# Hymba-style decoder step with PEER experts: one set of products for the sample values, residual transposed into PSUM and added at the end, gate loads moved ahead, and stores of the result by row tile

## The reference, cut to what matters

```python
xn = rms_norm(x, norm1_g)                       # 576 x 1024
q, k, v, glu = project(xn, w_in)                # 8 query heads, 2 key heads of 64
a = sliding_window_attention(q, k, v, sinks)    # prompt: blocks of 128; sample: 128 cached keys + 8 new
c = conv_module(glu)                            # depthwise conv, layernorm, swish, pointwise
h = x + concat(rms_norm(a), rms_norm(c)) @ w_out
xt = rms_norm(h)
# PEER: 8 heads, each takes 16 of 128 x 128 experts by two lists of 128 keys
idx, gate = product_key_top16(xt @ wq, keys)
hu  = sum_d u[idx, d] * xt[d]                   # first table
act = gelu(hu) * gate
y   = h + sum_k act[k] * v[idx[k], :]           # second table
```

## Time and profile before

| | us |
|---|---|
| median of 3 runs (lowest, highest) | 1780.7 (1778.49, 1786.08) |
| profiled execution | 1786.37 |
| its span | 1784.6 |
| PE busy | 1659.4 (93%) |
| VectorE (DVE) busy | 1432.4 (80%) |
| ScalarE (ACT) busy | 781.7 (44%) |
| GpSimd (POOL) busy | 574.3 (32%) |

### The profile page before, as it was taken

One profiled execution on the slowest core, in us unless ns is written; L12 is line 12 of the kernel. 1 busy time (PEld: TensorE's weight loads), 2 busy tenths in 40 slices (PEclk: granted clock), 3 DMA queues, 4 the chain that ended last, 5 costly groups with the idle time before them and its releaser, 6 DMA issues.

```text
span 1784.6 us, 23135 instructions
## 1 busy us (share of the span) xinstructions
PE 1659.4 (93%) x8377; PEld 1417.5 (79%) x8377; DVE 1432.4 (80%) x2697; ACT 781.7 (44%) x1310; POOL 574.3 (32%) x395
## 2 busy tenths in 40 slices
PE   7886989899999899998999999998999989999997
PEld 5765645578699899998999999997777778777786
DVE  2558577865787687889889999838989989899897
ACT  3221230331135444447889999843333333333332
POOL 0000000000000232334555655524545556456462
PEclk9999999989999999999999999999999999999999
DMA  6110603115345689897999999999999999999996
GB/s 198 48 48 0 75 12 103 63 49 178 104 130 142 229 284 303 291 296 261 366 365 397 406 385 370 358 379 377 403 404 395 403 402 375 404 403 404 403 384 214
DMA packets 155320, 482.39 MB, mean 270 GB/s; under 512 B 25999, under 2 KB 43087, under 8 KB 153031
## 3 DMA queue, kind: packets, MB, share of 16 engines
q1 hardware_dynamic: 99911, 279.57, 44.6%
q0 software_dynamic: 55296, 201.35, 29.9%
HBM read 426.17 MB, written 54.42 MB: 269 GB/s over the span
## 4 chain that ended last, share of the span: by engine, by line
PE 49%; DMA 19%; DVE 19%; ACT 7%; issue 4%; SPq 1%; DVEq 0%; ACTq 0%
PE ps L786 19%; DMA raw<-in_v 12%; DMA gelu_matrix<-gest 7%; PE ps L936 6%; PE ps L740 6%; DVE acc L1656 5%; PE ps L550 5%; PE ps L566 4%; DVE lo L1491 3%; PE ps L914 3%; ACT hi L1053 2%; DVE cacc L1346 2%; ACT Gs L1228 2%; DVE al L1778 2%; ACT gA L1212 1%
## 5 line engine op out<-in xcount | busy, mean ns | idle before, releaser
L1274 POOL DMA_INDIRECT ring<-in_u,idx x192 | 280.7, 1462 | 953.5 <-DVE ijg L1632 579.8
L1491 DVE TENSOR_TENSOR lo<-raw,hi 128x1024 fp32r<-128x1024 f32 x256 | 312.9, 1222 | 154.1 <-ACT hi L1053 152.6
L1053 ACT ACTIVATE hi<-raw 128x1024 fp32r<-128x1024 f32 x256 | 270.6, 1057 | 361.0 <-DMA raw<-in_v 185.8
L1274 POOL DMA_INDIRECT ring<-in_v,idx x192 | 292.2, 1522 | 226.0 <-DVE acc L1656 216.4
L786 PE MATMUL ps<-xh,hi 128*128 128x384 f32 x1024 | 350.6, 342 | 7.8 <-DVE lo L1491 7.8
L786 PE MATMUL ps<-xh,lo 128*128 128x384 f32 x1024 | 343.6, 336 | 0.0
L786 PE MATMUL ps<-xl,hi 128*128 128x384 f32 x1024 | 343.6, 336 | 0.0
L936 PE MATMUL ps<-hi,ah 128*128 128x512 f32 x768 | 243.5, 398 | 29.3 <-DVE al L1778 26.7
L1656 DVE SCALAR_TENSOR_TENSOR acc<-ring,hu,acc 128x1024 f32<-128x1024 f32 x192 | 245.1, 1277 | 0.1
L936 PE MATMUL ps<-lo,ah 128*128 128x512 f32 x768 | 238.9, 393 | 0.0
L936 PE MATMUL ps<-hi,al 128*128 128x512 f32 x768 | 238.3, 392 | 0.0
(11 more groups left out here) (211 smaller groups left out, 1978.9 us busy)
## 6 DMA issues: line engine op xcount, KB each, us to landing
raw<-in_uT SPq DMA_DIRECT2D x128, 512.0 KB, 6.8
raw<-in_v SPq DMA_DIRECT2D x128, 512.0 KB, 9.2
wring<-in_wblk SPq DMA_DIRECT2D x58, 512.0 KB, 3.6
gelu_matrix<-gest SPq DMA_DIRECT2D x64, 384.0 KB, 8.9
gate_matrix<-Gs SPq DMA_DIRECT2D x16, 1536.0 KB, 8.5
Gl<-gate_matrix SPq DMA_DIRECT2D x64, 384.0 KB, 11.5
gel<-gelu_matrix SPq DMA_DIRECT2D x64, 384.0 KB, 8.8
wring<-in_wblk SPq DMA_DIRECT2D x16, 256.0 KB, 2.6
```

The lines of the kernel that those rows point to most:

```text
L1053: nc.scalar.activation(hi[:, s % 2, :], raw[:, s % RAWS, :], ACT.Copy).then_inc(s_hi, 1)
L1274: pool.indirect_dma_start(ring[:, r % SLOTS, :], None, table, bass.IndirectOffsetOnAxis(idx[:, t, c:c + 1], 0)).then_inc(g_in[r % SLOTS], 16)
L1491: nc.vector.tensor_tensor(lo[:, s % 2, :], raw[:, s % RAWS, :], hi[:, s % 2, :].bitcast(F32), ALU.subtract).then_inc(s_lo, 1)
```

## The change

1. `sample_values`: eight matmuls, one for each sequence, with all 128 value columns and the weights of both key heads (64 columns of output), and one matmul of 512 columns that adds the new values for all. Half of each result is not used: VectorE takes the rows and columns of each key head in a copy of its own.
2. The residual: TensorE transposes h into `ps[0..2]`, ScalarE copies it back over the dense part of `hT` (now by tokens), the first value products start the sums, and the residual is added by VectorE when PSUM is emptied, whole row tiles at a time. ScalarE has no part in that.
3. SyncE waits for the gate block and loads the first gates and the first GELU pair ahead of `after_u(123)`; the next three pairs follow one by one.
4. The gathered rows of v are all done by value tile 124 (`V_ROWS_END`), and the sample's upper half is released there.
5. The dense result is stored as three row tiles, each as soon as it is added.

```diff
+V_ROWS_END = NKEY - 4
 def v_rows(n):
-    return V_ROW0 + n * (NROW - V_ROW0) // NKEY
+    return V_ROW0 + min(n, V_ROWS_END) * (NROW - V_ROW0) // V_ROWS_END
...
+            sp.wait_ge(s_gst, 16 * NBLK)
+            load_gelu(0)
+            for b in range(0, NBLK, 2):
+                load_gates(0, b)
             for n in range(U_TAIL, NKEY):
                 after_u(n)
-                if n == U_TAIL + 1:
-                    sp.wait_ge(s_gst, 16 * NBLK)
-                    for b in range(0, NBLK, 2):
-                        load_gates(0, b)
-                    for k in range(EP):
-                        load_gelu(k)
+                if n - U_TAIL < EP - 1:
+                    load_gelu(n - U_TAIL + 1)
...
-            sp.wait_ge(s_yd, 2 * DTI)
-            sp.dma_start(y_d[0:DT, :].rearrange("(t p) d -> p t d", p=P), ring[:, 0:DTI, :]).then_inc(s_out, 16)
-            sp.wait_ge(s_out, 48)
+            for t in range(DTI):
+                sp.wait_ge(s_yd, t + 1)
+                sp.dma_start(y_d[t * P:(t + 1) * P, :], ring[:, t, :]).then_inc(s_out, 16)
+            sp.wait_ge(s_out, 16 * (2 + DTI))
...
                 for b in range(NDB):
-                    for g in range(NKV):
-                        grp, slot = b // 2, (b % 2) * 2 + g
-                        rows = slice(g * HD, (g + 1) * HD)
-                        c = grp * P + slot * 32
-                        nc.tensor.matmul(out[rows, b * 32:b * 32 + 32], cv[:, b, rows], PTb[:, c:c + 32],
-                                         start=True, stop=False)
-                        mm = nc.tensor.matmul(out[rows, b * 32:b * 32 + 32], vtok[0:NS, 4, rows],
-                                              PTb[0:NS, 512 + c:512 + c + 32], start=False, stop=True)
-                mm.then_inc(ready, 1)
+                    c = slice(b * 2 * 32, (b + 1) * 2 * 32)
+                    nc.tensor.matmul(out[:, c], cv[:, b, :], PTb[:, c], start=(b == 0), stop=False, skip_group_check=True)
+                nc.tensor.matmul(out[:, 0:512], vtok[0:NS, 4, :], PTb[0:NS, 512:1024], start=False, stop=True,
+                                 skip_group_check=True).then_inc(ready, 1)
...
             for t in range(DTI):
                 for c in range(DC):
-                    mm = nc.tensor.matmul(ps[t][:, c * P:(c + 1) * P], hT[:, c, t * P:(t + 1) * P], ident[:, :],
-                                          start=(c % 4 == 0), stop=False, skip_group_check=True)
+                    mm = nc.tensor.transpose(ps[t][:, c * P:(c + 1) * P], hT[:, c, t * P:(t + 1) * P], ident[:, :])
+                mm.then_inc(s_hr, 1)
...
+                    if n == 0:
+                        pe.wait_ge(s_hk, t + 1)
...
-                                                  b[:, n % 2, h * 512:(h + 1) * 512], start=False,
+                                                  b[:, n % 2, h * 512:(h + 1) * 512], start=(n == 0 and k == 0),
...
-                mm.then_inc(s_vd, 1)
+                    if n == NKEY - 1 or t == DTI - 1:
+                        mm.then_inc(s_vd, 1)
...
+            for t in range(DTI):
+                act.wait_ge(s_hr, t + 1)
+                nc.scalar.activation(hT[:, :, t * P:(t + 1) * P], ps[t][:, :].rearrange("p (c d) -> p c d", c=DC),
+                                     ACT.Copy).then_inc(s_hk, 1)
             for n in range(U_TAIL, NKEY):
                 step(n)
...
-            act.wait_ge(s_vd, NKEY)
-            act.wait_ge(g_used, NROW)
-            for t in range(DTI):
-                nc.scalar.activation(ring[:, t, 0:512], ps[t][:, 0:512], ACT.Copy).then_inc(s_yd, 1)
...
-            nc.vector.tensor_copy(ATb[:, :, P:GT].rearrange("p j (b s) -> p b j s", b=NDB),
-                                  p[:, 0:256].rearrange("p (b j s) -> p b j s", b=NDB, j=GQ)).then_inc(s_at, 1)
+            for g in range(NKV):
+                rows = slice(g * HD, (g + 1) * HD)
+                ins = nc.vector.tensor_copy(
+                    ATb[rows, :, P:GT].rearrange("p j (b s) -> p b j s", b=NDB),
+                    p[rows, 0:512].rearrange("p (b g j s) -> p b g j s", b=NDB, g=NKV, j=GQ)[:, :, g])
+            ins.then_inc(s_at, 1)
...
+                if n == V_ROWS_END:
+                    dve.wait_ge(g_used, NROW)
+                    dve.sem_inc(s_up, 1)
...
-            dve.wait_ge(g_used, NROW)
-            dve.sem_inc(s_up, 1)
-            dve.wait_ge(s_vd, NKEY)
-            for t in range(DTI):
-                nc.vector.tensor_copy(ring[:, t, 512:D], ps[t][:, 512:D]).then_inc(s_yd, 1)
             dve.wait_ge(s_mv, 16)
             nc.vector.tensor_tensor(acc[0:NS, 1, :], acc[0:NS, 1, :], xtok[0:NS, 0, :], ALU.add).then_inc(s_y, 1)
+            for t in range(DTI):
+                dve.wait_ge(s_vd, NKEY + t)
+                nc.vector.tensor_tensor(ring[:, t, :].rearrange("p (c d) -> p c d", c=DC),
+                                        ps[t][:, :].rearrange("p (c d) -> p c d", c=DC),
+                                        hT[:, :, t * P:(t + 1) * P], ALU.add).then_inc(s_yd, 1)
```

More of the change, by code:

```diff
@@ L393, in hymba_peer @@
         s_yd = sem("y_dense_copied")
+        s_hr = sem("residual_transposed")
+        s_hk = sem("residual_kept")
         s_ad = sem("act_chain")
```

## The result

| | before | changed |
|---|---|---|
| median of 17 runs, us | 1780.11 (1775.05 to 1786.08) | 1787.44 (1780.66 to 1789.79) |
| ratio | | 1.0031, 95% interval 1.0018 to 1.0044 |
| profiled execution, us | 1786.37 | 1780.66 |
| its span, us | 1784.6 | 1778.6 |

By the ratio the change makes the kernel 5.5 us slower (3.2 to 7.8), less than half a percent; the two medians lie 7.3 us apart. The two profiles say the contrary: the changed kernel's was taken of its shortest execution and before's of an execution as long as its longest. "Profile" is one execution, "runs" are the times of all.

The account below looks back on a forecast made before the run. The value loop was taken to be bound by DMA at 400 GB/s, not TensorE. Terms -6.8 + 0 + 5.0 + 7.8 - 5.8 = +0.2 us gave a median of 1780.9 us; 8-in-10 range 1771 to 1788 us.

Parts of the forecast that it names:

- Rival C: Change-over between loops: PE stays at 1.2 GHz through tiles 126 and 127; term +11, sum +6.2, 1786.9 us; chance 0.12.
- Rival D: Sample attention: sample values gain nothing, VectorE and ScalarE's chain being late by itself; sum +7.0, 1787.7 us; chance 0.06.
- sample values: Sample attention: 32 matmuls become 9, no half clock, VectorE's ranking starts earlier; -6.8 us (-4.0 to -7.2).
- residual: Residual products: transposes take half of 5.52 us of PE, ScalarE's copies run beside PE's work; 0 us (-0.5 to +1).
- order of SyncE: Change-over: late tiles and pair 60's store queue behind 8 gate loads, so PE stands still; +5.0 us (+2 to +11).
- rows: Value loop: rows ready at tile 124 move six gathers, 3.15 MB, into the DMA-full stretch; +7.8 us (0 to +8.5).
- end: After PE's end: sample add done earlier, three row-tile stores, span ends +4.4 to +5.2; -5.8 us (-4.5 to -6.5).
- Rival B: Change-over: reordered queue costs nothing, late tiles were waiting for pair 61's store; sum -4.8, 1775.9 us; chance 0.10.
- rival A: Value loop: the six rows ride free, the loop being a round trip; sum -7.6, 1773.1 us; chance 0.22.
- The sign named for it: Value loop: distance from first value product to PE's end some 8 us longer; unchanged would mean rival A.

Follow-up runs that it names:

- b2: Kernel before with the sample values alone changed; ratio to before 0.9969 (0.9957 to 0.9980).
- a0: The changed kernel again, no edit; ratio to before 1.0028 (1.0015 to 1.0041).
- a2: Changed kernel with SyncE's order of before (gates behind raw tile 127); ratio to before 0.9977 (0.9959 to 0.9996).
- a1: Changed kernel with gathered rows spread over 128 tiles as before, sample's add and store behind the row tiles; ratio to before 1.0002 (0.9984 to 1.0020).
- a3: Changed kernel with both the rows and SyncE's order as before; ratio to before 0.9946 (0.9926 to 0.9967).
- b4: Kernel before with the transposed residual and the stores by row tile alone, sample's add behind them; ratio to before 0.9976 (0.9964 to 0.9989).
- c2: Changed kernel with the wait left ahead of after_u(123), but gate loads behind after_u(124) as before; ratio to before 1.0012 (0.9997 to 1.0027).
- d2: a3 with only SyncE's wait for the gate block moved ahead of after_u(123); ratio to before 0.9960 (0.9944 to 0.9977).
- d1: a3 again, no edit, as partner of d2 on the same chip; ratio to before 0.9940 (0.9917 to 0.9962).
- a4: Changed kernel with gathered rows done by value tile 112 instead of 124, a dose test; ratio to before 1.0168 (1.0144 to 1.0193).

## Why the prediction was right, and by what it missed

The time is inside the range, and "within half a percent" held. But the sum was +0.2 us and the runs say +5.5. The median of 1787.44 us lies 0.6 us under the upper end of the range and outside the bounds of the forecast itself (1775 to 1786). The range reached so far up for rivals C and D, at 1786.9 and 1787.7, and both of them fell. That the range held is in part luck.

| term | predicted | profiles | runs |
|---|---|---|---|
| sample values | -6.8 | -7.7 (11 profiles with, 3 without) | -5.5 (b2) |
| residual | 0 | hidden | |
| order of SyncE | +5.0 | +8.0 from store to value; 2.9 MB, 7.2 us | +9.1 (a0, a2), +10.0 (a1, a3) |
| rows | +7.8 | +6 in the value loop | +6.0 (a0, a1), +6.9 (a2, a3) |
| end | -5.8 | -6.3 | -5.7 (b4, with the 1.4 us of the late sample add) |
| sum | +0.2 | about 0 | +4.8 |

The sum of the parts by runs, -5.5 - 5.7 + 9.5 + 6.5 = +4.8 us, agrees with the +5.5 of the whole. The sum by profiles is some 5 us lower. Each of its terms is inside the interval of the one by runs, and the stretch up to the last gate store scatters by 9 us from profile to profile; more than that I can't say of the rest.

*Sample values.* Right in each step: 2.88 us (predicted 2.7), no half clock, VectorE next with a wait of 1.99 us. Rival D falls, with b2.

*Residual.* Right: 2.78 us and 2.85 us, both beside other work.

*Order.* The chain of events came as predicted, each within about a microsecond: the gate store landed after 8.8 us (9.2 predicted, though for a reason that the other profiles don't bear out, see the last section), pair 60's buffer was free 24.1 us after the store (23.1), PE's gap was 11.1 us (10.2), the value loop started after 39.4 (39.2). **The step that failed is the size of the term: "5.8 less what earlier landing may give".** It measured 8.0 us from store to value over all profiles and 9.5 us by runs, give or take 3.1. I took 0.8 us off for earlier landing, which the chain of times had already been started from (1186 us): that was counted twice. The rest comes of the two ends of the difference. The stretch of 33.4 us that I started from is the longest of the seven profiles in the old order (mean 32.2), and the new order takes 39.4 to 40.9 us (mean 40.2) where 39.2 was predicted. I had also argued that the loop is bound by bytes, and then priced this part by the start of PE's work. Priced in bytes, 2.9 MB less move in the 44 us after the gate store, 7.2 us at 400 GB/s. Both prices are inside the uncertainty of the runs, which don't tell which is the better one. The loss also has two sources that I took for one: the empty engines while SyncE waits, and those when the loads of the value loop go out late. The wait alone is c2 against a2 (6.2 us, give or take 4.2) and d2 against d1 (3.6, give or take 5), weighted together 5.1 us, give or take 3.2 (each run by its ratio to before on its own chip). The gate loads ahead of the tiles are a0 against c2 (2.8, give or take 3.5) and a1 against d2 (7.5, give or take 4.3), together 4.7 us, give or take 2.7. So each is there, at some 5 us; the exact shares stay open.
Rival B falls: pair 61's store was what before waited for, and still the earlier tiles' delay came on top. Rival C falls: of the last two tiles only about the first nine matmuls of tile 126 ran at 1.2 GHz, the other 39 at 2.4. Half of that tile at 1.2 GHz, as predicted, is 2.1 us more and not the 2.3 that the sum took.

*Rows.* Right in mechanism and near in size (+6 to +7 for 7.8), and the dose test leaves no room for rival A: 19 more gathers, 9.96 MB, cost 24.9 us by runs, which is 400 GB/s. The sign named for it, a value loop some 8 us longer, came out as 4 us in the first profile and 6 in a0.

*End.* Right: 4.1 us from PE's end, predicted 4.4 to 5.2. Three lone stores of 2.6 us from -1.4 end at +6.4, not +6.8, a slip that changes nothing. The rule of the Trainium skill on 1 MiB per DMA ("DMA: Bandwidth & Descriptors", Rules for kernel authors) is not borne out as a reason against it here: b4, with three stores of half that, gains 4.3 us. The last store lands in 2.6 us where the single one took 6.6, and the two ahead of it are issued while VectorE still adds.

## What to carry to other kernels

Where a stage is bound by DMA, price what an edit adds to it in bytes: for the gathered rows 9.96 MB cost 24.9 us by runs, though no engine was busier. For a change of order ahead of such a stage, look at the DMA engines as well as at PE. Here a wait in the queue that issues the loads left them short of work, and by two pairs of runs it cost some 5 us, give or take 3, though the first value product came only 2 and 4 us later. In such a stage work that brings its own loads is best left where the loads have room: here doing it four tiles earlier cost 6 to 7 us and shortened the end by 1.4. And two single profiles can point the other way than the runs: here they said 6 us faster where 17 runs each said 5.5 us slower. The same holds for a stretch of one profile from which a sum starts.

## What was not expected of the hardware

I had let the changed order shorten the landing of the last gate store, since 1.4 MB no longer move beside it. The 8.8 us of the first profile, against 10.9 before, seemed to bear that out; the others hardly do. With 1.4 MB issued behind it the next issue that waits for the store came 10.9, 9.8, 9.4, 9.9, 8.8, 8.9 and 9.1 us after it (before and its second profile, b2, b4, a2, a3, d1). With nothing issued behind it, it came 8.8, 9.3, 9.0, 9.0, 9.0 and 9.0 us after it (changed, a0, a1, a4, c2, d2). The means are 9.5 and 9.0 us: a difference of half a microsecond at most a hint, beside a spread of 2 us, and not the 1.7 us that I had allowed for.
